# RWKV scan: decay blocks made inside the rounds by the hyperbolic tangent, in place of two batches of eight by the sigmoid

## What is computed

```python
lw = einsum("zblr,zrd->zbld", tanh(einsum("bld,zdr->zblr", xw, w1)), w2) + w0   # z: two directions
decay = exp(-exp(-softplus(-lw) - 0.5))        # = exp(-0.6065 * sigmoid(lw))

def rwkv7_scan(r, w, k, v, kk, a, S):          # per head, one token after the other
    sa = einsum("bhvk,bhk->bhv", S, -kk_t)
    S = S * w_t + sa * (kk_t * a_t) + v_t * k_t
    y_t = einsum("bhvk,bhk->bhv", S, r_t)
```

## Time and profile before

| | us |
|---|---|
| median of 3 runs | 2937.8 |
| lowest, highest | 2935.99, 2942.82 |
| the profiled execution's own time | 2936.99 |
| its span (first to last instruction of the profile) | 2935.2 |
| busy: PE, DVE, ACT, POOL | 2744.0, 1714.5, 1307.3, 109.9 |
| the loop ahead of the scan | 2233.2 to 2257.8 |
| the scan | 2257.8 to about 2650 |
| its batch of eight decay blocks | 2433.7 to 2448.4 |

### The profile page before, as it was taken

One profiled execution on the slowest core, in us unless ns is written; L12 is line 12 of the kernel. 1 busy time (PEld: TensorE's weight loads), 2 busy tenths in 40 slices (PEclk: granted clock), 3 DMA queues, 4 the chain that ended last, 5 costly groups with the idle time before them and its releaser, 6 DMA issues.

```text
span 2935.2 us, 58366 instructions
## 1 busy us (share of the span) xinstructions
PE 2744.0 (93%) x24236; PEld 2195.7 (75%) x24236; DVE 1714.5 (58%) x2670; ACT 1307.3 (45%) x2108; POOL 109.9 (4%) x152
## 2 busy tenths in 40 slices
PE   8999999999999999998888999998998888877998
PEld 7887788888877888677667877776454776764986
DVE  6756567577565775312566777644442564565885
ACT  6645566465565665322343522334212544433333
POOL 0000000000000000000000000000000232320000
PEclk9999999999999999997998999999998999998999
DMA  6554445555543554542001344331210000003443
GB/s 259 187 186 161 144 146 190 190 178 183 190 168 115 180 181 150 200 158 89 2 3 52 117 150 151 114 115 47 93 58 29 4 4 25 4 4 115 158 146 112
DMA packets 50390, 349.40 MB, mean 119 GB/s; under 512 B 5840, under 2 KB 5840, under 8 KB 9808
## 3 DMA queue, kind: packets, MB, share of 16 engines
q1 hardware_dynamic: 49680, 343.56, 32.7%
q0 software_dynamic: 448, 2.11, 0.2%
HBM read 344.61 MB, written 1.05 MB: 118 GB/s over the span
## 4 chain that ended last, share of the span: by engine, by line
PE 78%; DVE 13%; ACT 4%; issue 3%; DMA 1%; DVEq 0%; POOL 0%; ACTq 0%; SPq 0%; POOLq 0%
PE psum L170 76%; DVE arena L98 3%; DVE ring_low L87 2%; PE psum L175 2%; DVE arena L87 2%; DVE wide L87 1%; ACT wide L138 1%; ACT w_high L144 1%; DVE ring L87 1%; DVE wide L98 1%; ACT arena L144 0%; ACT arena L140 0%; DVE arena L94 0%; ACT L138 0%; DVE small L106 0%
## 5 line engine op out<-in xcount | busy, mean ns | idle before, releaser
L170 PE MATMUL psum<-x_both,w_high 128*128 128x512 f32 (+1 forms) x2800 | 843.6, 373 | 9.7 <-DVE arena L87 7.8
L87 DVE TENSOR_TENSOR ring_low<-ring,w_high 128x2048 fp32r<-128x2048 f32 (+3 forms) x254 | 560.2, 2206 | 428.6 <-ACT w_high L144 413.9
L144 ACT ACTIVATE w_high<-ring 128x2048 fp32r<-128x2048 f32 (+3 forms) x254 | 469.5, 1848 | 531.5 <-PE psum L170 236.5
L170 PE MATMUL psum<-x_both,ring_low 128*128 128x256 f32 (+1 forms) x2104 | 604.3, 301 | 0.0
L170 PEld LDWEIGHTS psum<-x_both,w_high 128*128 128x128 f32 x2800 | 493.8, 189 | 107.1 <-issue 18.4
L170 PE MATMUL psum<-w_high,x_both 128*128 128x512 f32 (+2 forms) x1440 | 453.4, 391 | 10.6 <-issue 10.0
L170 PEld LDWEIGHTS psum<-x_both,ring_low 128*128 128x128 f32 x2104 | 397.7, 189 | 32.0 <-DVE x_both L98 0.8
L170 PE MATMUL psum<-wide,ring 64*64 64x64 f32 (+3 forms) x2864 | 322.9, 298 | 13.1 <-issue 6.7
L170 PEld LDWEIGHTS psum<-w_high,x_both 128*128 128x128 f32 x1440 | 278.0, 197 | 74.9 <-issue 20.7
L170 PEld LDWEIGHTS psum<-wide,ring 64*64 64x64 f32 (+2 forms) x2864 | 206.3, 152 | 120.8 <-issue 97.0
L170 PE MATMUL psum<-ring_low,x_both 128*128 128x512 f32 (+2 forms) x720 | 279.3, 388 | 0.0
(11 more groups left out here) (195 smaller groups left out, 3037.8 us busy)
## 6 DMA issues: line engine op xcount, KB each, us to landing
ring<-in_f_gu SPq DMA_DIRECT2D x88, 1024.0 KB, 4.8
ring<-in_w_mod SPq DMA_DIRECT2D x48, 1024.0 KB, 5.0
ring<-in_fu SPq DMA_DIRECT2D x44, 1024.0 KB, 4.9
ring<-in_f_dn SPq DMA_DIRECT2D x40, 1024.0 KB, 4.8
ring<-in_w_in SPq DMA_DIRECT2D x28, 1024.0 KB, 4.7
ring<-in_fd SPq DMA_DIRECT2D x20, 1024.0 KB, 4.9
ring<-in_rkvr SPq DMA_DIRECT2D x12, 1024.0 KB, 4.9
ring<-in_w_out SPq DMA_DIRECT2D x8, 1024.0 KB, 4.8
```

The source lines that it names most:

```text
L87: self.done(self.eng.tensor_tensor(o, a, b, op), then)
L144: self.done(self.eng.activation(o, i, ACT.Copy, scale=scale), then)
L170: ins = self.eng.matmul(o, l, r, start=a, stop=z)
```

## The change

- **Function.** sigmoid(x) is made as 0.5 tanh(0.5 x) + 0.5: the activation is Tanh with scale 0.5, and a new DVE instruction (`decay_dve`, one tensor-scalar with two constants, in place on a 128x512 block in SBUF) finishes it.
- **Ahead of the scan.** Only the two blocks of direction 0, tb 0 (one per group) are made, in items 0 and 1 of the loop; items 2 to 7 have only the values and the bonus.
- **In the scan.** The table `DECAYS` names one (direction, tb) for each odd round 1 to 13. In such a round each group makes its half: PE right behind `p1` (bank 4g), ACT one slot behind its copy `yy`, DVE behind `q2`. The batch at round 8 is gone. So 14 blocks are made in the scan, two in each of seven rounds.
- **Waits.** `cum` waits for a decay block only in even rounds, for that of its own group. The block's bank is taken behind `us` or `y` (DVE), and `s` of the same group, which is next on that bank, waits for the Tanh (`lw_t`).
- **Weights.** Slot 3 comes free in round 5 instead of ahead of the scan, slot 4 in round 13 instead of round 8.

In the built program PE and POOL have as many instructions as before, DVE has 16 more. ACT has three fewer table loads: that between the loop and round 0, and the two around the batch at round 8. Between the small Tanh ahead of the loop and the end of the scan no load is left.

The diff, cut to what the steps speak of:

```diff
@@ signals
-        LWS = [(z, tb, n) for z in TWO for tb in FOUR for n in TWO]
-        lw_mm = signal("lw_mm", [x for x in LWS if x[1:] != (3, 1)])
-        lw_ok = signal("lw_ok", LWS)
+        DECAYS = {1: (0, 1), 3: (0, 2), 5: (0, 3), 7: (1, 1), 9: (1, 0), 11: (1, 3), 13: (1, 2)}
+        LWS = [(0, 0)] + list(DECAYS.values())
+        RW2_ENDS = ((0, 3), (1, 2))
+        lw_mm = [signal(f"lw_mm{g}", [x for x in LWS if not (g and x in RW2_ENDS)]) for g in TWO]
+        lw_t, lw_ok = [[signal(f"{n}{g}", LWS) for g in TWO] for n in ("lw_t", "lw_ok")]
@@ helpers
-            T.bank(b, lw_ok[z, tb, n])
...
-            A.act(LW[:, tb, 512 * n:512 * n + 512], bank(b), ACT.Sigmoid, lw_ok((z, tb, n)))
...
+            T.bank(b, lw_t[g][z, tb])
...
+        def decay_act(A, z, tb, g, b):
+            A.eng.wait_ge(*decay_done(z, tb, g))
+            A.act(LW[:, tb, 512 * g:512 * g + 512], bank(b), ACT.Tanh, lw_t[g]((z, tb)), scale=0.5)
+
+        def decay_dve(D, z, tb, g):
+            x = LW[:, tb, 512 * g:512 * g + 512]
+            D.eng.wait_ge(*lw_t[g][z, tb])
+            D.tsc(x, x, 0.5, 0.5, ALU.mult, ALU.add, lw_ok[g]((z, tb)))
@@ scan_pe
-                if n == 8 and g == 0:
-                    decay_pe(T, 1)
                 if new:
                     z, c = n // 8, chunk(n)
-                    te.wait_ge(*lw_ok[z, 3, 1])
+                    if n % 2 == 0:
+                        te.wait_ge(*lw_ok[g][z, c // 2])
...
                 one_straight(False, (n, "p1"), tq, it1)
+                if n in DECAYS:
+                    decay_pe(T, *DECAYS[n], g, 4 * g)
                 yield
@@ scan_act
-                if n == 8 and g == 0:
-                    decay_act(A, 1)
...
                 take(yy, (n, "p1"))
-                yield from rest(4)
+                yield
+                if n in DECAYS:
+                    decay_act(A, *DECAYS[n], g, 4 * g)
+                yield from rest(3)
@@ scan_dve (behind q2 and the moments)
+                if n in DECAYS:
+                    decay_dve(D, *DECAYS[n], g)
                 yield
@@ rwkv_pe, rwkv_act, rwkv_dve
-                decay_item_pe(T, 0, tb, g, 4 + i % 4)
+                if tb == 0:
+                    decay_pe(T, 0, 0, g, 4 + g)
...
-            A.act(small[:, 216:217], ident[:, 0:1], ACT.Sigmoid)
+            A.act(small[:, 216:217], ident[:, 0:1], ACT.Tanh)
...
-                decay_item_act(A, 0, tb, g, 4 + i % 4)
+                if tb == 0:
+                    decay_act(A, 0, 0, g, 4 + g)
...
             for i in range(8):
+                if i < 2:
+                    decay_dve(D, 0, 0, i)
```

More of the change, by code:

```diff
@@ L2968, in columns, with decay_done, decay_pe @@
             return x.rearrange("p (v u) t -> p u v t", u=2)
-        def decay_item_pe(T, z, tb, n, b):
+        def decay_done(z, tb, g):
+            return w_free["rw2", z] if g and (z, tb) in RW2_ENDS else lw_mm[g][z, tb]
+        def decay_pe(T, z, tb, g, b):
             te = T.eng
@@ L2975, in decay_item_pe @@
             s = slice(64 * z, 64 * z + 64)
-            T.bank(b, lw_ok[z, tb, n])
-            T.mm(bank(b), TH[s, 128 * tb:128 * tb + 128], w[s, 512 * n:512 * n + 512], True, False)
-            T.mm(bank(b), C("ones")[s, :], w[s, 1024 + 512 * n:1536 + 512 * n], False, True,
-                 w_free(key) if tb == 3 and n == 1 else lw_mm((z, tb, n)))
-        def decay_item_act(A, z, tb, n, b):
-            A.eng.wait_ge(*(w_free["rw2", z] if tb == 3 and n == 1 else lw_mm[z, tb, n]))
-            A.act(LW[:, tb, 512 * n:512 * n + 512], bank(b), ACT.Sigmoid, lw_ok((z, tb, n)))
-        def decay_pe(T, z):
-            for i, (tb, n) in enumerate(ITEMS):
-                decay_item_pe(T, z, tb, n, i)
-        def decay_act(A, z):
-            for i, (tb, n) in enumerate(ITEMS):
-                decay_item_act(A, z, tb, n, i)
+            T.bank(b, lw_t[g][z, tb])
+            T.mm(bank(b), TH[s, 128 * tb:128 * tb + 128], w[s, 512 * g:512 * g + 512], True, False)
+            T.mm(bank(b), C("ones")[s, :], w[s, 1024 + 512 * g:1536 + 512 * g], False, True,
+                 w_free(key) if g and (z, tb) in RW2_ENDS else lw_mm[g]((z, tb)))
+        def decay_act(A, z, tb, g, b):
[5 more added lines that the diff above has]
+            D.tsc(x, x, 0.5, 0.5, ALU.mult, ALU.add, lw_ok[g]((z, tb)))
         def scan_pe(T, g):
```

## The result

The kernel before took 2937.44 us (median of 17 runs, 2932.16 to 2949.23), the changed one 2942.82 us (17 runs, 2939.14 to 2948.89), on the same chip. The ratio is 1.0019, with a 95% interval of 1.0010 to 1.0028: 5.4 us slower. That is on the edge of what I had said a measurement can tell from no change; with 17 runs a side the interval lies clear of 1. The profiled execution of the changed kernel took 2943.62 us, with a span of 2941.8.

What follows compares the result with a forecast made beforehand. The scan was taken as bound by a dependent chain in PE's order, the loop ahead by PE. Terms -7.8 - 15.0 + 23.8 (14 blocks) + 0.7 + 0.7 = +2.4 us on 2936.99 gave 2939.4, rounded to 2939; range 2928 to 2950.

Steps and rivals of the forecast that it cites:

- Loop, -7.8: Loop ahead of the scan: items 2 to 7 lose their blocks, DVE sets 1.52 us an item, gain 7.8 us.
- Rival D: Loop ahead: thinner items bring the clock's fall forward, gain 6.0 instead of 7.8 us; inside the forecast's range, no own chance.
- Batch, -15.0: Round 8: removing the batch of blocks and its table load gains 15.0 us, ends 14.2 to 15.6.
- PE's price of a block, 1.73: Odd scan rounds: each of the 14 blocks costs PE 1.73 us before any cover.
- Cover, 0.25 for group 0 and none for group 1: Behind `p1`: a block hides up to 0.25 us of `p2`'s wait in group 0, nothing in group 1.
- Bank behind `y`, 0.7: Rounds 5, 7 and 13, group 0: the block's bank waits 0.25 us for DVE to take `y`, 0.7 in all.
- The Tanh's 0.2 in group 1: Group 1's blocks: the Tanh makes group 0's `e2` 0.6 us later; DVE's slack leaves 0.2 us of cost.
- rival B: Scan: ACT's order exposes the Tanh, 0.69 us more a block, +8 to 2947, or 2950 with tensor-scalars; chance 0.2.
- Tensor-scalars, 0.7: Scan on DVE: 14 tensor-scalars cost 0.05 us each, 0.7 in all, within 0 to 7.7.
- Waits for instructions, "rounded down" for them: Scan: blocks may now and then cover PE's "issue" waits, so 2939.4 us was rounded down to 2939.
- rival C: Scan: PE's instruction waits fall elsewhere, either sign: 2954 or 2928 us; chance 0.05 each.
- Weights: nothing waits: Weight slot 4 comes free in round 13; a load lands in 6 us, before it is wanted, so no cost.

Runs made afterwards that it cites:

- e4: Kernel before with direction 0 made as before and only direction 1 spread over rounds 7, 9, 11, 13, without the batch at round 8: ratio 1.0012.
- e7: Changed kernel with the Tanh of the 14 in-scan blocks over 64 of 512 columns: ratio 1.0018.
- e8: Changed kernel with DVE's tensor-scalar of the 14 in-scan blocks over 64 of 512 columns: ratio 1.0016.
- e5: Kernel before with 32 small matmuls (128 PE instructions) added ahead of the loop that precedes the scan: ratio 1.0055.
- e6: Changed kernel with 32 small matmuls added ahead of the loop that precedes the scan: ratio 1.0078.
- e3: Changed kernel with each in-scan block put in front of `p1` of its group, not behind it: ratio 1.0015.
- e2: Kernel before with each of its 16 decay blocks made by one matmul in place of two: ratio 0.9968.
- e9: Kernel before with 32 small matmuls (128 PE instructions) added behind the batch of round 8: ratio 1.0001.
- e10: Changed kernel with 32 small matmuls added ahead of the first `cum` of round 8: ratio 1.0035.
- e1: Changed kernel with each decay block made by one matmul in place of two: ratio 0.9992.
- e11: Kernel before with one matmul a decay block, plus 8 small matmuls behind the loop and 40 behind the batch of round 8: 2919.05 us, ratio 0.9931.
- e12: Changed kernel with the two weight loads that the last decay block sets free held back until `m3` of round 15: ratio 1.0012.

## Why the prediction was right or wrong, point by point

The time (2942.82 against 2939, within 2928 to 2950) and the sign of the sum were right; of the three outcomes the likeliest one was "same", and by the boundary of 0.2% the measured 1.0019 is still in it, just. Behind the number some steps failed and offset each other, so a part of that nearness is luck.

- **Loop, -7.8: right.** 7.55, with DVE's 1.52 us an item as worked out. Rival D (the clock falls in the loop) didn't come.
- **Batch, -15.0: right as far as it can be told.** 14.9 by the marks of rounds 7 and 8, 12.5 by those of e4.
- **PE's price of a block, 1.73: mis-sized.** It was read in the batch, where a block follows a block. Between other work it is 1.91 to 1.92, as the row of the loop said and I had at hand. 14 x 0.18 = 2.5 us.
- **Cover, 0.25 for group 0 and none for group 1: too small.** PE's waits for other engines fell by 5.2 us, of which about 1 lay in the batch. The blocks take the place of waits for DVE and ACT all over the round, not only of the one right behind them.
- **Bank behind `y`, 0.7: a little less.** PE waits 0.15 us for it in rounds 5 and 7 of group 0 and in round 7 of group 1, 0.46 together, and not in round 13.
- **The Tanh's 0.2 in group 1, and rival B: not there.** Two waits that I had named appear in the trace, 0.32 for `s` above; e7 shows that they are worth nothing that can be measured.
- **Tensor-scalars, 0.7: right in sum.** About 1 us by e8, within its scatter. But one takes 0.67 us in the mean and not the 0.55 of the row that I went by the earlier trace rows; see below.
- **Waits for instructions, "rounded down" for them: the step that failed.** I took their sum as fixed at 30 us, gave rival C 0.1 and let it depend on chance places. They rose by 7.5 us (by 9.6 and 4.1 in e7 and e8, with the same PE program). Place can do that much, as e5 and e6 show (9 to 10 us for half a packet). The collision of round 13 is 1.1 to 2.3 of it. The third cause is only argued: behind a block all other engines have caught up, so PE runs without a wait until the packet is out. How the 7.5 split among these three stays open, and for rounds with a block I found no rule of the place. The sum is also no cost by itself: in e3 it was 29.3 in a scan only 1 us shorter.
- **"Weights: nothing waits": wrong.** I asked only whether the moved loads land in time. They do. But PE's next instruction packet, a DMA transfer too, began only at 2589.89, when they had all but landed (4.9 and 6.2 us from their issue). In the kernel before they were sent at 2447.73, right behind the batch, and the wait at 2455.84 was 1.18 us.
- **The clock**: 20.5 us of low clock at the scan's start became 13.7, a gift of 2.3 us (round 0) that no term of mine had. And the agreement that I read from the 0.57 of round 0 (rival D) was too quick: PE was not idle there, it was busy for 15.38 of these 20.50 us.

The tests that I had set: even rounds moved by +0.1, +0.2 and +0.8 (rounds 6, 4, 10) but also by -1.1 and +2.0 (rounds 2 and 8), and odd rounds of group 0 grew by 3.2, 4.8, 6.5, 4.0, 3.6 and 2.7. By my mark for even rounds C was under way. By that for odd rounds (more than 4.5) rounds 3 and 5 pointed to B, which e7 rules out: in these two rounds "issue" alone took 1.3 and 2.5 us more than before, so the marks don't separate the two rivals.

The Trainium skill ("Runtime: NRT & Kernel Launch", Instruction fetch mechanics) calls the cost of crossing a 16 KiB boundary "mostly hidden". By this case's trace 34 of 81 packets of the scan are felt, for 27.8 us of 365.66, and in e5 for 40.9 of 375.58. The measurement decides.

## What to carry to other kernels

Where PE runs many small matmuls, its instruction stream is a resource of its own. Work moved into such a stretch can take the place of waits on other engines and meet waits for instructions in their stead; count both sums in the profile before and after, for they nearly cancelled here (-5.2 and +7.5), and don't take one of them alone for the cost. When a loop's length is close to a multiple of 256 PE instructions, the places of the packets' ends hold for the whole loop. A few idle matmuls ahead of it are then a legitimate tool: they were worth 10 us on e2, nothing on the kernel before (e9), and cost 5 us on the changed one (e10), so they have to be tried and not reckoned. An edit that only takes instructions out can cost as much as it saves, so judge an edit by two versions at different places.

A transfer that is set free by moved work starts at the new place: ask what stands on the DMA engines there, PE's own instructions included. And the saving that all theories agreed on was not to move the block but to make it half as long.

## What the runs showed of the hardware that I had not expected

**The fall of the clock mostly stands behind a wait of PE, but few such waits bring one.** Besides the scan's start, every stretch of 3.4 us at the lower level in the scans of the kernel before (three), the changed one (one) and e2 (four) began within 2 us behind a wait of PE of 1.4 us or more: in the kernel before at 2562.7, behind waits of 1.28 and 1.45 us at 2556.99 and 2561.31; in the changed one at 2593.0, behind the 2.73. One of the eight, in the kernel before at 2617.3, followed a wait for POOL and not for instructions. In e1 and e9 three began behind shorter ones (0.4 to 1.3 us). In e11 and e12 there was none. Counted over the scans of all fourteen profiles, without each one's start, 22 of 32 stretches at the lower level began during a wait of 1.4 us or more or within 2 us behind it, but of 62 waits of that length 40 had none behind them, that of 2.49 us in e9 among these. So a long wait can cost more than its own length; what decides is open.

**DVE's tensor-scalar depends on POOL.** Alone it takes 0.43 us at 128x512 (round 1, below), and up to 0.90 when a POOL product is under way at its start (round 1's other one). Of the 14 in the changed kernel's scan, the nine that start 0.1 to 0.3 us into a POOL product of 0.7 us took 0.72 to 0.90; the other five took 0.43. At 128x64 it is still 0.20 to 0.67. Timelines of DVE, then of POOL, in the changed kernel:

```profile
2282.88 0.90 DVE L94 TENSOR_SCALAR wide<-wide 128x512 f32<-128x512 f32 x1
2296.28 0.43 DVE L94 TENSOR_SCALAR wide<-wide 128x512 f32<-128x512 f32 x1
```

```profile
2282.76 0.73 POOL L150 TENSOR_TENSOR ring<-ring,cx 128x256 f32<-128x256 f32 x1
```

The Trainium skill ("Trainium Architecture — The Big Picture", What this means for kernel authors) says that only DVE and GpSimd contend on the engine side, by "an exclusive lock"; the trace agrees, with 0.47 us of delay in this case.
